# Input statistics in the natural layout, the first modulation vectors by channel halves, recurrent heads normalised one by one, in a hybrid encoder block

## The reference

```python
mods = jnp.split(silu(c) @ w_ada + b_ada, 9)          # (1024,) @ (1024, 9*1024)
h = rmsnorm(x, norm_g[0]) * (1 + sc1) + sh1
x = x + 0.5 * g1 * (silu(gate) * up) @ w_ffn1_out     # gate, up = split(h @ w_ffn1_in)
...
o = outs[0] + outs[1]                                 # 4 recurrent heads of 128 channels
o = o * rsqrt(mean(o * o, over the head's channels) + EPS) * hgrn_norm_g * silu(g)
mixed = concat([o, o_attn]) @ w_mix_out
```

## Time and profile before

| | |
|---|---|
| median of 3 runs | 1118.34 us (1118.32 to 1121.73) |
| the profiled execution: its own time | 1118.59 us |
| its span in the profile | 1116.4 us |
| TensorE busy | 1081.5 us, 97% of the span |
| VectorE busy | 553.5 us, 50% |
| ScalarE busy | 400.6 us, 36% |
| mean granted TensorE clock | 0.992 of full speed |
| first feed-forward matmul | 44.21 us after the span's start |

### The profile page before, as it was taken

The page is one execution under the profiler, slowest core; times in us unless marked ns, Lnnn a source line. Parts: engine busy times, 40 slices in busy tenths (PEclk is TensorE's granted clock), DMA queues, the critical chain, the costliest instruction groups (busy, mean ns, idle before and its releaser), DMA issues.

```text
span 1116.4 us, 12625 instructions
## 1 busy us (share of the span) xinstructions
PE 1081.5 (97%) x5035; PEld 873.1 (78%) x5035; DVE 553.5 (50%) x629; ACT 400.6 (36%) x498; POOL 38.6 (3%) x31
## 2 busy tenths in 40 slices
PE   7699999999999999999998999999999999999998
PEld 4488888888888887778885778788888888888886
DVE  5955545454445487335449894477222223242323
ACT  5542324232322253225246765244221212132221
POOL 0000000000000050000000000050000000000000
PEclk9899999999999999999999999999999999999999
DMA  8854655555345543222310001123233232323212
GB/s 336 310 189 163 213 173 203 180 196 188 113 179 197 155 132 113 76 76 76 113 39 1 1 1 39 38 76 113 84 105 101 86 113 75 113 77 111 93 57 76
DMA packets 89480, 133.46 MB, mean 120 GB/s; under 512 B 10569, under 2 KB 73413, under 8 KB 89318
## 3 DMA queue, kind: packets, MB, share of 16 engines
q1 hardware_dynamic: 89208, 130.82, 34.3%
q10 hardware_dynamic: 238, 2.17, 0.5%
HBM read 128.78 MB, written 4.19 MB: 119 GB/s over the span
## 4 chain that ended last, share of the span: by engine, by line
PE 85%; DVE 9%; ACT 3%; issue 2%; SPq 0%; DMA 0%; POOL 0%; ACTq 0%; DVEq 0%; POOLq 0%
PE bank L1317 26%; PE bank L1319 25%; PE bank L1318 25%; DVE tmod L956 1%; PE bank L1682 1%; PE bank L1405 1%; DVE h_lo L962 1%; DVE w_lo L882 1%; DVE qp_both L1201 1%; DVE a_diag L1218 1%; ACT lg L771 1%; DVE z L1201 1%; PE bank L1665 1%; PE bank L1424 1%; PE bank L1393 1%
## 5 line engine op out<-in xcount | busy, mean ns | idle before, releaser
L1317 PE MATMUL bank<-h_hi,w_hi 128*128 128x512 f32 x912 | 357.3, 392 | 3.4 <-DVE w_lo L882 2.0
L1319 PE MATMUL bank<-h_hi,w_lo 128*128 128x512 f32 x912 | 355.4, 390 | 0.0
L1318 PE MATMUL bank<-h_lo,w_hi 128*128 128x512 f32 x912 | 355.4, 390 | 0.0
L882 DVE TENSOR_TENSOR w_lo<-w_raw,w_hi 128x2048 fp32r<-128x2048 f32 x83 | 192.3, 2316 | 300.2 <-ACT w_hi L572 300.2
L572 ACT ACTIVATE w_hi<-w_raw 128x2048 fp32r<-128x2048 f32 x83 | 158.9, 1915 | 482.8 <-PE bank L1319 479.5
L1317 PEld LDWEIGHTS bank<-h_hi,w_hi 128*128 128x128 f32 x912 | 171.6, 188 | 42.6 <-issue 2.9
L1319 PEld LDWEIGHTS bank<-h_hi,w_lo 128*128 128x128 f32 x912 | 171.6, 188 | 36.0
L1318 PEld LDWEIGHTS bank<-h_lo,w_hi 128*128 128x128 f32 x912 | 171.7, 188 | 35.1
L1317 PE MATMUL bank<-a_hi,w_hi 128*128 128x512 f32 x352 | 137.3, 390 | 0.0
L1319 PE MATMUL bank<-a_hi,w_lo 128*128 128x512 f32 x352 | 137.0, 389 | 0.0
L1318 PE MATMUL bank<-a_lo,w_hi 128*128 128x512 f32 x352 | 137.0, 389 | 0.0
(11 more groups left out here) (194 smaller groups left out, 900.4 us busy)
## 6 DMA issues: line engine op xcount, KB each, us to landing
w_raw<-in_w_ffn_in SPq DMA_DIRECT2D x44, 1024.0 KB, 5.6
ada<-in_w_ada SPq DMA_DIRECT2D x30, 1024.0 KB, 4.9
w_raw<-in_w_ffn_out SPq DMA_DIRECT2D x22, 1024.0 KB, 4.8
w_raw<-in_w_mix_in SPq DMA_DIRECT2D x11, 1024.0 KB, 5.1
ada_first<-in_w_ada SPq DMA_DIRECT2D x6, 1024.0 KB, 17.8
x_nat<-in_x SPq DMA_DIRECT2D x1, 2048.0 KB, 15.4
bias_shear<-rowpad ACTq DMA_DIRECT2D x1, 2048.0 KB, 10.1
w_raw<-in_w_mix_in SPq DMA_DIRECT2D x8, 256.0 KB, 4.3
```

The source lines that it names most:

```text
L882: ve.tensor_tensor(w_lo[n % 2][:], raw[n % 2][:], as_f32(w_hi[n % 2][:]), ALU.subtract).then_inc(wlo_done, 1)
L1317: te.matmul(out_ap, wh, xh, start=first, stop=False)
L1318: te.matmul(out_ap, wh, xl, start=False, stop=False)
L1319: return te.matmul(out_ap, wl, xh, start=False, stop=last)
```

## The change

At the start:

- The loads have a new order. Each piece of `w_ada` now holds 512 channels of both the scale and the shift vector (two transfers of 0.5 MB), so four pieces give both vectors for channel tiles 0 to 3 (the first half), four more for tiles 4 to 7. Weight 0 is loaded second, weight 1 after the fifth piece, the input in two halves between. `c`, `ident` and the small rows are issued by ScalarE.
- The mean squares are taken on `x_nat`, whose partitions are tokens: ScalarE squares with a sum along the row (`rms0`), four instructions of 128 x 1024. The scaled input `xn` is made in that layout, two tiles by each of ScalarE and VectorE, and TensorE turns `xn`; it also turns `x_nat` (`turn_x`), four tiles before and four after the last matmul of the first two stages.
- Both first stages are split at the channel half (`first_hi`, `first_low`). ScalarE makes `h_hi` and the unrounded `tmod` with scale and shift in one instruction each.
- The bias rows are one matmul of 8 x 512, spread by the transfer that stores them.

At the recurrent heads: each head's squares are summed by a matmul with 128 x 128 ones (`o_sum(h)`), with its own root and reciprocal of 128 x 512 (`rto`); the spread is gone, and the attention half of output stage 1 is done before the heads' part of stage 0.

The diff, cut to its core:

```diff
 # SyncE
-            for kk in range(4):
-                load_first(0, kk)
-            sp.dma_start(x_nat[:], x[0].rearrange("(t p) d -> p t d", p=P)).then_inc(x_loaded, 16)
-            for kk in range(4):
-                load_first(1, kk)
+            load_first(0, 0)
+            load_w(0)
+            for kk in range(1, 4):
+                load_first(0, kk)
+            for half in range(2):
+                sp.dma_start(x_nat[:, 2 * half:2 * half + 2, :],
...
+            load_first(1, 0)
+            load_w(1)
+            load_first(1, 1)
+            load_first(1, 2)
+            sp.wait_ge(acc_step, 2)
+            load_first(1, 3)
 # ScalarE
+            a.dma_start(c_row[:], c.rearrange("o (t q) -> (o t) q", q=P)).then_inc(c_loaded, 16)
+            a.dma_start(ident[:], ident_c.ap()).then_inc(consts_loaded, 16)
...
+            for t in range(TT):
+                a.wait_ge(x_loaded[t // 2], 16)
+                sc.activation(xn[:, t, :], x_nat[:, t, :], ACT.Square, accum_out=rms0[:, 0, t:t + 1]).then_inc(xsq_done, 1)
...
+            def first_h(d, out, src):
+                return sc.activation(out[:, d, :], src, ACT.Identity, scale=fac[:, 0, d:d + 1], bias=modv[:, d:d + 1])
...
+            for d in range(4):
+                a.wait_ge(xn_tr, d + 1)
+                first_h(d, h_hi, bank[4 + d][:]).then_inc(norms[0].hi, 1)
+            whi(1)
+            for d in range(4):
+                first_h(d, tmod, bank[4 + d][:]).then_inc(norms[0].t, 1)
...
+            for d in range(4, DT):
+                first_h(d, h_hi, tmod[:, d, :]).then_inc(norms[0].hi, 1)
+                a.wait_ge(norms[0].hi, d + 1)
+                first_h(d, tmod, tmod[:, d, :]).then_inc(norms[0].t, 1)
+            for d in range(2, DT):
+                evac_x(d)
+            a.wait_ge(rowpad_done, 1)
+            a.dma_start(shear.rearrange("(p e) -> p e", p=P)[:, 0:QH * ROW].rearrange("p (h j) -> h p j", h=QH),
+                        row8[:].unsqueeze(1).to_broadcast([QH, P, ROW])).then_inc(bias_stored, 16)
             a.wait_ge(lb_dve, 3)
             sc.activation(lb_t[:, 3:5, :], lb_t[:, 1:3, :], ACT.Exp).then_inc(lb_exp, 1)
 # VectorE
+            first_chunk(0, 0)
             wlo(0)
+            first_chunk(0, 1)
...
+            first_chunk(0, 2)
+            first_chunk(0, 3)
+            first_finish(0)
...
+            first_chunk(1, 0)
             wlo(1)
+            for d in range(4):
+                first_lo(d)
+            for kk in range(1, 4):
+                first_chunk(1, kk)
+            first_finish(1)
+            for d in range(4, DT):
+                first_lo(d)
 # TensorE
+            first_hi(0, range(4))
+            pe.wait_ge(wlo_done, 2)
+            first_hi(1, range(4))
...
+            first_low(0, range(4))
...
+            ada_sum(1, ada_acc1)
+            turn_x(2)
+            turn_x(3)
+            first_hi(0, range(4, DT))
+            first_hi(1, range(4, 6))
+            first_low(0, range(4, DT)).then_inc(stage_done, 1)
+            first_hi(1, range(6, DT))
+            first_low(1, range(4, DT)).then_inc(stage_done, 1)
+            for d in range(4, DT):
+                turn_x(d)
 # TensorE, recurrent heads
-            for h in range(HH):
-                values(h)
-                if h + 2 < HH:
-                    far2(h + 2)
...
+            values(0)
+            far2(2)
+            values(1)
+            far2(3)
+            o_sum(0)
+            values(2)
+            o_sum(1)
+            values(3)
+            o_sum(2)
...
+            out_part(0, range(HH, DT), (0,))
+            o_sum(3)
+            out_part(0, range(HH, DT), (1,))
+            pe.wait_ge(wlo_done, N_MIXOUT + 2)
+            out_part(1, range(HH, DT))
```

More of the change, by code:

```diff
@@ L579, in _ @@
             a.dma_start(relb[0:NB, :], rel_bias).then_inc(bias_consts, 16)
+            sc.activation(warm[:, 2:3], eps_t[:], ACT.Sqrt)
+            whi(0)
             a.wait_ge(rows_T, 1)
             sc.activation(vec[:], bank[0][:, 0:P], ACT.Copy).then_inc(vec_done, 1)
[L583 to L588, removed]
+            a.wait_ge(bias_mm, 1)
@@ L676, in ffn_act @@
                 whi(n1)
+                if not last:
+                    a.wait_ge(bias_stored, 16)
                 ahi(0, 0)
@@ L1395, in ada_sum @@
                 ins.then_inc(ada_mm, 1)
[L1397 to L1399 removed]
+            pe.wait_ge(pool_set, 7)
             pe.wait_ge(bias_consts, 48)
[L1401 to L1408 removed]
+            te.matmul(bank[1][0:QH, :], relb[:], table[:], start=True, stop=True).then_inc(bias_mm, 1)
@@ L1422, in _, with turn @@
-            for q in range(DT):
-                pe.wait_ge(norms[0].sq, q + 1)
-                ins = te.matmul(norms[0].bank[:], ones[:], sq[:, q, :], start=(q == 0), stop=(q == DT - 1))
-            ins.then_inc(norms[0].ss, 1)
-            pe.wait_ge(xT_act, DT)
-            ada_sum(1)
+            def turn(dst, src, d):
+                for t in range(TT):
+                    ins = te.transpose(dst[:, t * P:(t + 1) * P], src[:, t, d * P:(d + 1) * P], ident[:])
+                return ins
@@ new lines, in turn_x, with first_hi @@
+            def turn_x(d):
+                if d < 2:
+                    pe.wait_ge(xn_ev, d + 1)
+                else:
+                    pe.wait_ge(xT_act, d - 1)
+                turn(bank[6 + d % 2], x_nat, d).then_inc(x_tr, 1)
+            pe.wait_ge(xn_act, 2)
+            pe.wait_ge(xn_dve, 2)
+            pe.wait_ge(ada_out, 1)
+            pe.wait_ge(sink_done, 1)
+            for d in range(4):
+                turn(bank[4 + d], xn, d).then_inc(xn_tr, 1)
+            def first_hi(u, tiles):
+                for k in tiles:
+                    pe.wait_ge(norms[0].hi, k + 1)
+                    for cc in range(2):
+                        col = slice(k * 2 * P + cc * P, k * 2 * P + (cc + 1) * P)
+                        te.matmul(bank[2 * u + cc][:], w_hi[u][:, col], h_hi[:, k, :], start=(k == 0), stop=False)
+                        te.matmul(bank[2 * u + cc][:], w_lo[u][:, col], h_hi[:, k, :], start=False, stop=False)
@@ new lines, in first_low @@
+            def first_low(u, tiles):
+                for k in tiles:
+                    pe.wait_ge(norms[0].lo, k + 1)
+                    for cc in range(2):
+                        col = slice(k * 2 * P + cc * P, k * 2 * P + (cc + 1) * P)
+                        ins = te.matmul(bank[2 * u + cc][:], w_hi[u][:, col], h_lo[:, k, :],
+                                        start=False, stop=(k == DT - 1))
+                return ins
+            pe.wait_ge(vec_done, 1)
+            pe.wait_ge(rowpad_done, 1)
```

305 lines of the change are left out of this document (165 added, 140 removed).

## The result

The changed kernel takes 1142.31 us (median of 4 runs, 1140.85 to 1143.91) against 1119.37 for the kernel before (4 runs on the same chip, 1118.32 to 1121.73). The ratio is 1.020 with a 95% interval of 1.018 to 1.023: 2% slower, where no change was forecast, and outside the forecast range. The profiled execution took 1140.9 us, its span is 1138.7, 22.3 more than before.

A forecast was written before the change was run, and what follows sets the result against it. TensorE, busy 97% of the span, was taken to bound the kernel. 1118.6 plus 6.8 us at the start minus 6.7 at the heads gave 1118.7, written as 1118.8 us; range 1113.5 to 1123.

The forecast's parts named there:

- the stored bias: Bias store starting near 66 instead of 35: costed at nothing, since a weight held back about 10 us would still come in time.
- ScalarE's queue at `pair(1)`: Start: `whi(2)` and `silu` wait behind `xT` copies, Exp and loads; `pair(1)` at 73.8 instead of 68.6, some 8 us idling.
- The first `first_hi`: Start, first stage's first-half matmuls on TensorE: the first was forecast near 32.
- rival, C: Start: `c` lands late, at 9 instead of 3, `pair(1)` some 4 later, 1123 us; chance 0.14.
- the landings of the large transfers: Start: first piece of `w_ada` near 5.6, weight 0 near 8.5, input near 21.8, last piece near 35.5.
- the first matmuls: Start: the 16 matmuls of `first_hi(0)` end between 35.5 and 37.3; 37.3 taken, half clock at first.
- The half clock at `pair(1)`: TensorE restarts at half clock after idling before `pair(1)`: 1.6 us more.
- Table loads: ScalarE's table loads on the new path: 1.28 us each, without the skill's added drain of 1.38.
- rival D: Three table loads on the new start path cost double, 3.8 us more, 1122.6 us; chance 0.03.
- The heads: Recurrent heads: sums, spread and half clock removed, four float32 sums added; net 6.7 us less on TensorE, VectorE slack 0.4.
- Rival E: Recurrent heads: reciprocals too slow, each root starts later, 3 us lost, 1121.7 us; chance 0.09.
- Rival A: Start's loss at `pair(1)` and heads' gain cancel, 1115.5 to 1121.5 us; chance 0.56.

The follow-up runs named there:

- experiment 2: Changed kernel with each bias row on 16 partitions, stored behind `whi(1)` by eight transfers of 16 partitions each: 1120.85 us, ratio 1.001 to the kernel before.
- experiment 4: Kernel before with only the 8 x 512 bias matmul and the store from eight partitions, at the store's old place: 1137.7 us, ratio 1.016.
- experiments 7 and 8: experiment 2 with its store as sixteen transfers of 8 partitions: from another eight partitions each time (7, 1129.98 us), or all from the same eight (8, 1145.22 us).
- experiment 6: Experiment 5 with the loads of `c` and `ident` moved back to the head of SyncE's queue: 1110.9 us, ratio 0.992 to the kernel before.
- Experiment 5: experiment 2 with ScalarE reordered: Exp and SiLU table load in earlier idle time, no table loads in first turn, last four `xT` copies after first `silu`: 1111.27 us.
- experiment 3: Kernel before with the recurrent heads' part of the change alone: 1113.56 us, ratio 0.993.

## Why the prediction was wrong

**The step that failed** is that of the stored bias: "so I cost it at nothing; were a weight held back by as much as that store took before, about 10 us, it would still come in time". The bound was taken from the old store, with 128 source partitions and pieces of 16 KB; the new one has 8 partitions, a difference that the change names and the prediction did not price. It takes about 41 us, not 10, and the weight issued beside it landed after 34.6.

The overlap behind the bound was sound: `pair(2)` could have begun at 100.3, 5.7 us after its weight, so the weight had to land by 94.6, and issued at 78.67 it would by the old 5.6 have landed at 84.3, with 10.3 us to spare. It was held back by 29.0. The excess of 18.7 shows as the 18.52 us of idling. With 1.5 of half clock behind it (eight matmuls took 3.34 us, to 122.33, for 1.8) it cost 20 us: experiment 2 takes it out (20.9 of span), experiment 4 puts it in alone (17.3).

The Trainium skill has the rule that speaks against the change (DMA: Bandwidth & Descriptors, Why a DMA increments its semaphore by 16 and not by 1): a transfer is shared by the largest number of engines, up to sixteen, that divides the outermost size of both its patterns. With eight rows outermost that is eight, and the trace agrees: 0.47 of the sixteen, where the store is alone. The other factor of two is measured by experiments 7 and 8, and its cause stays open. That a weight's share on those eight engines took turns with the store's pieces is a reading of the windows (0.81 busy at 171 GB/s from 80 to 85, when both run, and 0.48 at 89 GB/s from 90 to 95, when the weight is still under way); no row names the engine of a piece, so that part is argued, not shown.

**ScalarE's queue at `pair(1)`** was right in kind and nearly in size. `whi(2)` and `silu` stood behind all copies to `xT`, the Exp and three table loads, 7.93 us of idling (8 forecast), at 76.08 (73.8 forecast). Two sources give 2.0 of the 2.3 us between. The first `first_hi` is at 33.40 for about 32. `cact` came at 7.12 where about 3 was assumed (ScalarE's two small loads landed beside SyncE's large ones), but experiment 6 shows that this rival, C, is at most part of it: with `c` early, the first piece of `w_ada` (5.6 forecast) was used only at 7.32 and weight 0 (8.5 forecast) at 10.46, and the turned input came 0.9 earlier (29.31 for 30.18). So the landings of the large transfers were put too early as well. And the pairs `h_hi`, `tmod` took 1.56 from start to start for 1.4, four times.

One error hid another: the first matmuls were put at half clock (end at 37.3), but ran at full clock (0.227 apart) from 33.4 and ended near 37.2. The half clock at `pair(1)` cost 2.4, not 1.6. Experiment 5 removes the queue and gets back 8.0 of span, 9.6 in the medians, where the prediction's terms, 8 of idling and 1.6 of half clock, give 9.6.

**Table loads** cost 1.28 and no more: 73.56 + 1.28 = 74.84, and the `silu` starts at 74.85. The further drain that rival D allowed for does not show. Rival D is out.

**The heads** gave 7.1 for 6.7, in the changed kernel and in experiment 3 alike. VectorE kept up, as forecast with a slack of 0.4: it was busy without a break from the first of four reciprocals of 3.35 us, at 717.39, to the last `h_lo`, and TensorE did not idle. Rival E is out.

**The sum, with what was measured:** the start 7.5 later and 2.4 of half clock, the second stall 18.7 and 1.5, make 30.1, and the `values` matmul of 670.60 is at 699.89, 29.3 later. The 0.8 between fits in direction what the clock did elsewhere: before that matmul it fell to half for 3.4 us twice in the kernel before (from 600.4 and from 614) and once in the changed one (from 511.2). The heads take 7.1 off: 22.2, and the spans differ by 22.3. Rival A, both cancel, is what experiment 2 shows once the store is mended: 1120.85 against 1120.39, where 1118.8 against 1118.6 was forecast. That this comes out so near is in part luck, since the start costs 9.3 there (7.3 later and 2.0 of half clock) and not 6.8, and one fall of the clock elsewhere (from 489.6) instead of two hides some of it.

## What to carry to other kernels

When an edit changes where a transfer's data stand, price the transfer anew, by how many partitions it is read from, even if its bytes and its deadline stay the same; "it isn't needed for long" holds for its own data, not for the other transfers on the same DMA engines. This weight stream, with one buffer of lead, could take a delay of 10 us and got 29. In the profile the sign is a DMA share that sits near a half or another fraction of sixteen at a low rate, and an issue on a queue that takes microseconds instead of tenths. And look at what is behind a late engine before mending it: `c` 4 us earlier gained less than one, ScalarE's order 8 or more.

## What the runs showed of the hardware

- Transfers with 8 source partitions kept the sixteen DMA engines 0.46 to 0.47 busy, those with 16 partitions 0.91.
- A store read from the same eight partitions throughout, each row 128 times over, moved 51 to 54 GB/s, by one transfer or by sixteen; read from another eight with each transfer it moved 104, at the same busy share. Whether the repeated row, the few partitions or the order of the targets makes it slow stays open.
- Beside such a store a 1 MB weight landed after 34.6 us and not 7.0 (5.6 over the kernel before), and SyncE's issues took 4.22 and 13.80 us and not 0.37.
- Issues behind a slow store hold their engine: twelve of 128 KB took ScalarE 15.16 us or 32.73, by the rate at which the store drained, where single ones take about 0.3.
